# Final RMSNorm: two of nine row tiles scaled on GpSimd and ScalarE in place of VectorE

## The chip, the cores and the metric

One core of one Trainium2 chip. The metric is the device time of one execution in microseconds (us), the median of three runs. The whole program is one launch.

## The reference, cut to what matters

The program is one step of a decoder layer on 1024 prompt rows and 8 sample rows of width 1024: a mixer (pooling and retention), a mixture of 32 experts, and at the end the final norm of every row. All of it stays as it is; what the change touches is the last line:

```
x  = x + mixed @ w_out
x  = x + hier_moe(rmsnorm(x, g_ffn))
y  = rmsnorm(x, g_final)          # x * 1/sqrt(mean(x*x) + 1e-6) * g_final, per row
```

Each output row is the row times one number of its own (the inverse root of its mean square) times a vector of 1024 weights that is the same for all rows.

## The kernel before, in words

The 1032 rows are nine tiles: eight of 128 prompt rows and one of the 8 sample rows. `ORDER` (L576) takes the sample tile first, so that place n = 0 is the 8 rows and places 1 to 8 are prompt tiles 0 to 7. Up to the last stage the kernel is bound by TensorE's products in fp32 split in two parts. The experts' results are added row by row to `sum_d` in DRAM by indirect transfers that GpSimd (POOL) issues (L1415). When all of them have landed, POOL raises `parts_ready` (L1444), and the last stage begins:

- SyncE (SP) issues nine loads, `sum_d` to the tile of `x2` in SBUF, in the order n = 0 to 8 (L677 to L679), each with a semaphore of its own, `rows_in[n]`. Then SP issues the stores of the outputs in the order n = 0 to 8 (L680 to L684): before each it waits for `y_done`, which counts the scalings done. The last tile is stored in two halves of 512 columns. At the end SP waits for all stores (L685).
- ScalarE (ACT) squares each tile as it lands, with the row's sum of squares as a side result (L834, `Square`, output thrown away), and takes the square root of the means once for each group of tiles (L839, helper L354). The groups are `NORM_GROUPS` (L585): n = 0 to 2, 3 to 5, 6 and 7, and 8. `root3_done` counts the groups.
- VectorE (DVE) waits for a group's root, works out the inverse root in five short instructions on a few columns (`rsqrt_columns`, L163 to L167), and then scales the group's tiles in place: one `scalar_tensor_tensor` for each tile, (x times the row's number) times `gfin_b` (L1355, in `scale_rows`); the last tile takes two, by halves. `TAIL` (L586) is the list of these steps. `gfin_b`, the final weights on every partition, was loaded long before.
- POOL has nothing to do in this stage; TensorE neither.

Each engine executes its instructions in order; SP's queue also, so a store whose wait isn't met holds back all stores behind it.

Two places outside the last stage are needed to follow the prediction. In the mixer stage POOL multiplies 128x256 gates by 128x256 weights (L2182) and adds two 128x256 tiles (L2193), both `tensor_tensor` on fp32 in SBUF, while DVE forms the low parts of weights (L1915, `tensor_tensor` on two SBUF tiles of 128x512) or masks keys (L2136, L2138, the same operation on two SBUF tiles).

Of the kernel before, what the change touches and what calls it, by code (L numbers as in the profile page):

```python
# [25 lines left out]
F32 = mybir.dt.float32  # L26
# [4 lines left out]
ALU = mybir.AluOpType  # L31
ACT = mybir.ActivationFunctionType
AX = mybir.AxisListType.X

P = 128
D = 1024
KT = D // P
SEQ, NB, NTOK = 1024, 8, 1032
NT = 9
CH = SEQ // P  # L40
TC = NTOK // 3
H = 4
# [133 lines left out]
def step_kernel(nc, x_prompt, x_sample, state_pool, state_ret, g_mix, w_in, w_pool, pool_scale, ret_gn,  # L176
# [10 lines left out]
    with ExitStack() as ctx:  # L187
        def sem(name):
            return ctx.enter_context(nc.semaphore(name))
# [9 lines left out]
        small = whole.place("small", [P, 96], F32)  # L199
# [3 lines left out]
        at_W = whole.at  # L203
# [50 lines left out]
        x2 = rh.place("x2", [P, NT, D], F32)  # L254
# [82 lines left out]

        gfin_b = rc.place("gfin_b", [P, D], F32)
        junk_f = rc.place("junk_f", [P, D], F32)

        SS, MS, RS = 0, 9, 18
        HX, TX = 27, 36
# [9 lines left out]
        def root_of_means(act, a, b):  # L352

            return act.activation(small[:, MS + a:MS + b], small[:, SS + a:SS + b], ACT.Sqrt,  # L354
                                  bias=small[:, EPSC:EPSC + 1])
# [24 lines left out]
        rows_in = [sem(f"rows_in{t}") for t in range(NT)]  # L380
        raw_in = [sem(f"raw_in{i}") for i in range(3)]
        misc_in = sem("misc_in")
        gains_in = sem("gains_in")
# [14 lines left out]
        y_out = sem("y_out")  # L398
# [22 lines left out]
        S = {**by_pe, **by_act, **by_dve, **by_pool, **by_sp}  # L421
# [8 lines left out]
        def after(n):  # L430

            return max(n, 0) + 1 if isinstance(n, int) else n + 1

        def carried(eng, who):

            eng.sem_inc(carrier[who], 1)
# [28 lines left out]
        def is_first(t, n):  # L465
            return isinstance(t, int) and t < n
# [42 lines left out]
        def up_weights(sp, e, s):  # L509

            for j, w in enumerate((w1, w3)):
                sp.dma_start(w13[s][:, j, :, :].rearrange("p k f -> p (k f)"),
                             of_expert(w, e).rearrange("(p k) f -> p (k f)", p=P)).then_inc(w13_in[s], 16)

        def down_weights(sp, e, s):

            sp.dma_start(w2t[s][:, :, :].rearrange("p i n -> p (i n)"),
                         of_expert(w2, e).rearrange("(p i) n -> p (i n)", p=P)).then_inc(w2_in[s], 16)
# [4 lines left out]
        def blocks(eng, step):  # L523

            for s in range(ROUND):
                step(s, s, 0)
            with eng.Fori(1, ROUNDS) as g:
                for s in range(ROUND):
                    step(ROUND * g + s, s, g)
            for s in range(NE - ROUND * ROUNDS):  # L530
                step(ROUND * ROUNDS + s, s, ROUNDS)
# [5 lines left out]
        def expert_of(s, g):  # L537

            return 8 * (s % 4) + 2 * g + s // 4
# [36 lines left out]
        ORDER = [CH] + list(range(CH))  # L576

        def rows_of(n):
            return slice(0, NB if ORDER[n] == CH else P)

        def halves_of(n):

            return (slice(0, D),) if n < NT - 1 else (slice(0, 512), slice(512, D))

        NORM_GROUPS = ((0, 3), (3, 6), (6, 8), (8, 9))  # L585
        TAIL = [step for g, (a, b) in enumerate(NORM_GROUPS)  # L586
                for step in [("norm", g)] + [("scale", n) for n in range(a, b)]]

        def columns(t):

# [2 lines left out]
        def load_mixed(sp, t):  # L593
            s = t % 2
            if t >= 2:
                sp.wait_ge(S["ct_mm"], after(2 * (t - 1)))

            sp.wait_ge(mix_out[s], 16 * ((5 - s) * (H - 1) + 1) + 16 * (t // 2))
            if t == CH:
                sp.dma_start(mi[s][0:NB, :], mixed_d[SEQ:NTOK, :]).then_inc(mi_in[s], 16)  # L600
            else:
                sp.dma_start(mi[s][:, :], mixed_d[t * P:(t + 1) * P, :]).then_inc(mi_in[s], 16)

        def load_x(sp, t):
            s = t % 2
            if t >= 2:
                sp.wait_ge(S["x2_done"], after(2 * (t - 1)))
            if t == CH:
                sp.dma_start(xr[s][0:NB, :], x_s).then_inc(xr_in[s], 16)
            else:  # L610
                sp.dma_start(xr[s][:, :], x_p[t * P:(t + 1) * P, :]).then_inc(xr_in[s], 16)
# [14 lines left out]
        def stage_c_sp(sp):  # L626
            sp.wait_ge(S["sum_done"], after(9 * H))
            sp.dma_start(gffn_b[:, :], g_ffn[0:1, :].to_broadcast([P, D])).then_inc(route_in, 16)
            sp.dma_start(wr[:, :, 0:4], w_grp[0].rearrange("(k p) g -> p k g", p=P)).then_inc(route_in, 16)
            sp.dma_start(wr[:, :, 4:36], w_exp[0].rearrange("(k p) g e -> p k (g e)", p=P))\  # L630
                .then_inc(route_in, 16)
            sp.dma_start(gffn8[0:KT, :], g_ffn[0].rearrange("(k p) -> k p", p=P)).then_inc(route_in, 16)
            for t in range(2, CH + 1):
                if t < CH:
                    load_mixed(sp, t + 1)
                load_x(sp, t)

            def weights(b, s, g):

                if is_first(b, 2):  # L640
                    sp.wait_ge(S["wo_used"], after(b + 1))
                elif is_first(b, 3):
                    sp.wait_ge(S["w_mm"], after(NT))
                    sp.wait_ge(xg_in[0], 16)
                elif is_first(b, 4):
                    sp.wait_ge(S["h2_done"], after(NT))
                    sp.wait_ge(x2_out, 16 * NT)
                else:
                    sp.wait_ge(S["up_used"], after(KT * (b - SLOTS + 1)))
                    if not isinstance(b, int):  # L650
                        carried(sp, "sp")
                up_weights(sp, expert_of(s, g), s % SLOTS)
                if is_first(b, 1):
                    return
                if not is_first(b, SLOTS + 1):
                    sp.wait_ge(S["down_used"], after(4 * (b - SLOTS)))
                    if not isinstance(b, int):
                        carried(sp, "sp")
                down_weights(sp, expert_of((s - 1) % ROUND, g - (s == 0)), (s - 1) % SLOTS)

            sp.dma_start(gfin_b[:, :], g_final.unsqueeze(0).to_broadcast([P, D])).then_inc(gains_in, 16)
            blocks(sp, weights)
            sp.wait_ge(S["down_used"], after(4 * (NE - SLOTS)))
            down_weights(sp, expert_of((NE - 1) % ROUND, ROUNDS), (NE - 1) % SLOTS)

            def more(b, i):
                sp.wait_ge(S["down_used"], after(4 * b))
                carried(sp, "sp")
                e = sp.value_load(spill[0:1, bass.ds(i + SPILL, 1)], min_val=0, max_val=NE - 1)
                up_weights(sp, e, 0)  # L670
                down_weights(sp, e, 0)

            spilled(sp, more)


            sp.wait_ge(S["parts_ready"], after(1))
            for n, t in enumerate(ORDER):  # L677
                r = rows_of(n)
                sp.dma_start(x2[r, t, :], sum_d[t * P:t * P + r.stop, :]).then_inc(rows_in[n], 16)  # L679
            for n, t in enumerate(ORDER):  # L680
                dst = y_prompt[0, t * P:(t + 1) * P, :] if t < CH else y_sample.rearrange("b o d -> (b o) d")
                for half in halves_of(n):
                    sp.wait_ge(S["y_done"], after(n + 1 + half.start // 512))
                    sp.dma_start(dst[:, half], x2[rows_of(n), t, half]).then_inc(y_out, 16)  # L684
            sp.wait_ge(y_out, 16 * (NT + 1))  # L685


        def stage_c_act(act):
# [141 lines left out]
            for n in range(NT):  # L830
                r = rows_of(n)
                act.wait_ge(rows_in[n], 48 if n == CH else 32)
                act.wait_ge(S["sq3_done"], after(n))
                act.activation(junk_f[r, :], x2[r, ORDER[n], :], ACT.Square, scale=D ** -0.5,  # L834
                               accum_out=small[r, SS + n:SS + n + 1]).then_inc(S["sq3_done"], 1)
                for a, b in NORM_GROUPS:
                    if b == n + 1:
                        act.wait_ge(S["sq3_done"], after(b))
                        root_of_means(act, a, b).then_inc(S["root3_done"], 1)  # L839


        def three(pe, out, lhs, rhs, first, last):
# [525 lines left out]
        def stage_c_pool(pool):  # L1368
# [73 lines left out]
            for i in range(2):  # L1442
                pool.wait_ge(sum_out[i], 8 * NE)
            pool.sem_inc(S["parts_ready"], 1)  # L1444

        @block.sync
        def _(sp):
# [113 lines left out]
            tail(H - 1, lambda i: first_loads_c(sp, i))  # L1563
            sp.wait_ge(fixed_out, 16)
            stage_c_sp(sp)


# [15 lines left out]
        def _(act):  # L1583
# [125 lines left out]
            with act.Fori(1, H - 1) as h:  # L1709
                head(h, False, False)  # L1710
            head(H - 1, False, True)
            stage_c_act(act)


# [520 lines left out]
```

## Time and profile before

| | us |
|---|---|
| runs | 1058.55, 1060.94, 1061.08; median 1060.94 |
| profiled execution, its own time | 1059.97 |
| its span in the trace | 1058.2 |
| busy: TensorE, VectorE, ScalarE, GpSimd | 982.4, 739.5, 443.4, 217.7 |
| the last stage: first load issued, span's end | 1033.3, 1058.2 |

The profiled execution's own time is 1.8 us more than its span: what lies outside the first and last record. The last stage has no TensorE work, so the share of the whole says nothing of it; it is read from its own stretch of the trace.

### The profile page before, as it was taken

The page shows a single profiled execution, that of the slowest core. Times are in us where ns is not written, and L with a number is a line of the kernel's source. Part 1 is how long each engine was busy: PE and PEld are TensorE (multiplying, and loading weights), DVE is VectorE, ACT ScalarE, POOL GpSimd, SP SyncE. Part 2 cuts the span into 40 slices and gives each one's busy share as a digit, 9 for nine tenths or more (in the row PEclk, how much of TensorE's full clock was granted, in tenths as well). Part 3 has the DMA queues.
Part 4 walks back from the last instruction along what each step waited for, and adds up shares of the span by engine and source line. Part 5 has one row for each costly group of instructions (what it writes and reads, how often), then busy time and mean ns, then how long its engine had stood idle before and what let it go on. Part 6 is the DMA issues. An engine that isn't in the chain of part 4 may idle for free.

```text
span 1058.2 us, 16461 instructions
## 1 busy us (share of the span) xinstructions
PE 982.4 (93%) x5342; PEld 845.9 (80%) x5343; DVE 739.5 (70%) x1616; ACT 443.4 (42%) x738; POOL 217.7 (21%) x223
## 2 busy tenths in 40 slices
PE   5799999999989999999997999978999999999970
PEld 4798888988879888898875888857888888888850
DVE  5584457855568555684556555669999999999955
ACT  6422113011130111301112221136899888898854
POOL 0001221012200122011220000012444443454310
PEclk9899999999999999999998999989999999999995
DMA  7610205111051110501016443269999999999828
GB/s 251 227 30 26 65 21 168 41 39 52 26 162 41 34 57 26 172 31 60 11 64 220 165 160 119 103 242 386 388 391 401 393 393 390 393 395 388 299 35 324
DMA packets 74727, 190.24 MB, mean 180 GB/s; under 512 B 12503, under 2 KB 47555, under 8 KB 62227
## 3 DMA queue, kind: packets, MB, share of 16 engines
q1 hardware_dynamic: 61403, 159.66, 39.9%
q0 software_dynamic: 13248, 29.62, 9.6%
q8 instruction: 41, 0.67, 0.3%
q14 instruction: 35, 0.29, 0.1%
HBM read 167.43 MB, written 38.68 MB: 195 GB/s over the span
## 4 chain that ended last, share of the span: by engine, by line
PE 83%; DVE 8%; DMA 4%; issue 2%; ACT 1%; SPq 1%; DVEq 0%; POOLq 0%; ACTq 0%
PE bank L1866 17%; PE bank L844 11%; PE bank L846 11%; PE bank L845 11%; PE bank L871 10%; PE bank L1867 9%; PE bank L982 3%; PE bank L901 1%; PE bank L1749 1%; PE bank L1889 1%; DMA raw<-in_w_in_dram 1%; PE bank L1881 1%; PE bank L1877 1%; DMA hc<-const_head_tables_dram 1%; DVE x L1355 1%
## 5 line engine op out<-in xcount | busy, mean ns | idle before, releaser
L1233 DVE TENSOR_TENSOR w_lo<-w,w_hi 128x1024 fp32r<-128x1024 f32 x128 | 150.3, 1215 | 0.2 <-DVE vec L1195 0.2
L733 ACT ACTIVATE w_hi<-w 128x1024 fp32r<-128x1024 f32 x128 | 129.7, 1068 | 2.9 <-PE bank L846 2.9
L1866 PE MATMUL bank<-wvg_hi,hT_hi 128*128 128x512 f32 x256 | 104.3, 407 | 0.0
L844 PE MATMUL bank<-w_hi,xT_hi 128*128 128x512 f32 x256 | 102.9, 402 | 1.3 <-issue 1.3
L1866 PE MATMUL bank<-wvg_lo,hT_hi 128*128 128x512 f32 x256 | 101.0, 395 | 0.0
L1866 PE MATMUL bank<-wvg_hi,hT_lo 128*128 128x512 f32 x256 | 100.7, 393 | 0.0
L846 PE MATMUL bank<-w_hi,xT_lo 128*128 128x512 f32 x256 | 100.3, 392 | 0.0
L845 PE MATMUL bank<-w_lo,xT_hi 128*128 128x512 f32 x256 | 99.7, 390 | 0.0
L844 PE MATMUL bank<-hT_hi,wuqk_hi 128*128 128x344 f32 x288 | 95.4, 331 | 4.4 <-ACT line L1656 4.1
L1697 ACT ACTIVATE v<-bank 128x256 f32<-128x256 f32 x32 | 12.3, 383 | 201.2 <-PE bank L1867 201.2
L2193 POOL TENSOR_TENSOR mixed<-onorm,pgate 128x256 f32<-128x256 f32 x36 | 37.8, 1050 | 278.6 <-DVE onorm L2018 278.6
L845 PE MATMUL bank<-hT_lo,wuqk_hi 128*128 128x344 f32 x288 | 92.9, 323 | 0.0
L846 PE MATMUL bank<-hT_hi,wuqk_lo 128*128 128x344 f32 x288 | 92.7, 322 | 0.0
L2114 DVE SCALAR_TENSOR_TENSOR state<-state,small,bank 128x256 f32<-128x256 f32 x28 | 13.5, 480 | 109.2 <-PE bank L1889 109.0
L1238 DVE TENSOR_TENSOR w_lo<-w,w_hi 128x1024 fp32r<-128x1024 f32 x64 | 75.6, 1222 | 20.0 <-ACT w_hi L740 20.0
L1415 POOL DMA_INDIRECT sum_d<-y,icol x28 | 45.5, 1624 | 138.1 <-ACT y L770 125.3
L1867 PE MATMUL bank<-wvg_hi,hT_hi 128*128 128x256 f32 x256 | 71.8, 281 | 0.0
L1867 PE MATMUL bank<-wvg_hi,hT_lo 128*128 128x256 f32 x256 | 71.8, 280 | 0.0
L1867 PE MATMUL bank<-wvg_lo,hT_hi 128*128 128x256 f32 x256 | 71.8, 280 | 0.0
L2182 POOL TENSOR_TENSOR sg<-sg,gn_b 128x256 f32<-128x256 f32 x36 | 26.7, 741 | 191.5 <-ACT sg L1699 184.7
L740 ACT ACTIVATE w_hi<-w 128x1024 fp32r<-128x1024 f32 x64 | 64.6, 1066 | 0.0
L844 PEld LDWEIGHTS bank<-hT_hi,wuqk_hi 128*128 128x128 f32 x288 | 55.0, 191 | 8.0 <-ACT line L1656 4.7
(256 smaller groups left out, 2397.6 us busy)
## 6 DMA issues: line engine op xcount, KB each, us to landing
w<-in_w_dram SPq DMA_DIRECT2D x96, 1024.0 KB
raw<-in_w_in_dram SPq DMA_DIRECT2D x60, 256.0 KB, 3.2
xall<-in_x_prompt_dram SPq DMA_DIRECT2D x8, 512.0 KB, 7.0
mixed_d<-mixed POOLq DMA_DIRECT2D x32, 128.0 KB, 3.2
sample_state<-in_state_ret_dram SPq DMA_DIRECT2D x16, 256.0 KB, 3.6
out_dram<-sample_state SPq DMA_DIRECT2D x16, 256.0 KB, 4.4
mixed_in<-mixed_d SPq DMA_DIRECT2D x8, 512.0 KB, 4.3
x_again<-in_x_prompt_dram SPq DMA_DIRECT2D x8, 512.0 KB, 3.5
```

What stands on the lines that cost most here:

```text
L733: act.activation(hi, whole_w, ACT.Copy).then_inc(S["up_hi"], 1)
L740: act.activation(hi, whole_w, ACT.Copy).then_inc(S["down_hi"], 1)
L844: pe.matmul(out, lhs[0], rhs[0], start=first, stop=False)
L845: pe.matmul(out, lhs[0], rhs[1], start=False, stop=False)
L846: return pe.matmul(out, lhs[1], rhs[0], start=False, stop=last)
L871: mm = pe.matmul(banks[4 - 2 * s + n][:, :], mT[s][xi][:, k, :], wo[k][wi][:, n * 512:(n + 1) * 512], start=(k == 0 and xi + wi == 0), sto ...
L1233: dve.tensor_tensor(lo, whole_w, hi, ALU.subtract).then_inc(S["up_lo"], 1)
L1238: dve.tensor_tensor(lo, whole_w, hi, ALU.subtract).then_inc(S["down_lo"], 1)
L1415: pool.indirect_dma_start(out=sum_d, out_offset=bass.IndirectOffsetOnAxis(ap=index, axis=0), in_=yb[s2][:, :], in_offset=None, bounds_chec ...
L1866: g = pe.matmul(gates, x[xi], wvg[wi][:, 1:3, k, :], start=first, stop=last)
L1867: m = pe.matmul(v[:, 0:DV], x[xi], wvg[wi][:, 0, k, :], start=first, stop=last)
L2193: pool.tensor_tensor(mixed[s][:, :], onorm[:, :], pgate[:, :], ALU.add).then_inc(S["sum_done"], 1)
```

## The change

Tiles n = 3 and n = 4 (prompt tiles 2 and 3) leave DVE. POOL multiplies each, once its load has landed, by the final weights into a new buffer `by_g`, which lies where expert weights lay before; ACT multiplies it there by the row's inverse root, which DVE still works out with its group. ACT does so after its squares of all nine tiles, and waits until DVE has scaled four tiles (0, 1, 2 and 5), by which time the roots of the second group are there. DVE scales the other seven. The stores go in a new order: n = 0, 1, 2, 5, 6, 7, then 3 and 4 from `by_g`, then 8 in two halves. The loads keep their order.

```diff
+        by_g = nc.alloc_sbuf_tensor_at("x_by_gain", [P, 2, D], F32, offset=at_W)
+        BY_POOL = (3, 4)
+        STORED = [n for n in range(NT - 1) if n not in BY_POOL] + list(BY_POOL) + [NT - 1]
...
-                for step in [("norm", g)] + [("scale", n) for n in range(a, b)]]
+                for step in [("norm", g)] + [("scale", n) for n in range(a, b) if n not in BY_POOL]]
...
-            for n, t in enumerate(ORDER):
+            scaled = 0
+            for n in STORED:
+                t = ORDER[n]
                 dst = y_prompt[0, t * P:(t + 1) * P, :] if t < CH else y_sample.rearrange("b o d -> (b o) d")
+                if n in BY_POOL:
+                    i = BY_POOL.index(n)
+                    sp.wait_ge(S["sig_done"], after(9 * H + i + 1))
+                    sp.dma_start(dst, by_g[:, i, :]).then_inc(y_out, 16)
+                    continue
                 for half in halves_of(n):
-                    sp.wait_ge(S["y_done"], after(n + 1 + half.start // 512))
+                    scaled += 1
+                    sp.wait_ge(S["y_done"], after(scaled))
                     sp.dma_start(dst[:, half], x2[rows_of(n), t, half]).then_inc(y_out, 16)
...
+            for i, n in enumerate(BY_POOL):
+                act.wait_ge(S["y_done"], after(4))
+                act.wait_ge(S["sum_done"], after(9 * H + i + 1))
+                act.activation(by_g[:, i, :], by_g[:, i, :], ACT.Identity, scale=small[:, RS + n:RS + n + 1])\
+                    .then_inc(S["sig_done"], 1)
...
+            pool.wait_ge(gains_in, 32)
+            for i, n in enumerate(BY_POOL):
+                pool.wait_ge(rows_in[n], 32)
+                pool.tensor_tensor(by_g[:, i, :], x2[:, ORDER[n], :], gfin_b[:, :], ALU.mult).then_inc(S["sum_done"], 1)
```

## Rows read from the trace of the kernel before

**Rows 1.** The chain that ended last, its last pieces: start us, us, what

```profile
1034.12 4.37 DMA x<-sum_d
1038.51 1.16 ACT junk_f L834 x2
...
1040.97 3.66 DVE x L1355 x3
...
1045.42 3.68 DVE x L1355 x3
...
1049.86 2.48 DVE x L1355 x2
...
1053.10 0.75 DVE x L1355
1053.85 0.66 DVEq L187
```

**Rows 2.** Busy time by stretch of the last stage; last columns granted clock, DMA share, GB/s

```profile
1035.00:1041.00 6.00, 0.00 (x0) 0.00 (x0) 0.76 (x6) 4.55 (x8) 0.00 (x0) 0.50 0.99 384
1041.00:1046.00 5.00, 0.00 (x0) 0.00 (x0) 4.86 (x9) 4.61 (x10) 0.00 (x0) 0.50 1.03 415
1046.00:1051.00 5.00, 0.00 (x0) 0.00 (x0) 4.86 (x9) 2.26 (x6) 0.00 (x0) 0.50 1.02 415
1051.00:1052.00 1.00, 0.00 (x0) 0.00 (x0) 1.00 (x2) 0.00 (x0) 0.00 (x0) 0.50 0.76 307
...
1054.50:1055.00 0.50, 0.00 (x0) 0.00 (x0) 0.01 (x1) 0.00 (x0) 0.00 (x0) 0.50 0.74 279
...
1056.00:1056.50 0.50, 0.00 (x0) 0.00 (x0) 0.00 (x0) 0.00 (x0) 0.00 (x0) 0.50 0.29 111
```

**Rows 3.** The waits of SP's queue in the last 30 us: total, times, longest

```profile
SPq L684 <- DVE x L1355: 13.8, 10, 4.6
```

**Rows 4.** Timeline of the last stage: start us, us, engine, line, what

```profile
1028.96 1.55 POOL L1415 DMA_INDIRECT sum_d<-y,icol  x1 [7.84 <-ACT y L770]
...
1040.19 1.06 ACT L834 ACTIVATE junk_f<-x 128x1024 f32<-128x1024 f32 x1 [0.21 <-DMA x<-sum_d]
1040.38 0.16 DVE L165 TENSOR_TENSOR small<-small 128x3 f32<-128x3 f32 x1
...
1046.99 1.06 ACT L834 ACTIVATE junk_f<-x 128x1024 f32<-128x1024 f32 x1
```

**Rows 5.** Groups of the last stage by shape: busy us, mean ns, idle before

```profile
L1355 DVE SCALAR_TENSOR_TENSOR x<-x,small,gfin_b 128x1024 f32<-128x1024 f32 x7 | 8.6, 1277 | 0.1
L834 ACT ACTIVATE junk_f<-x 128x1024 f32<-128x1024 f32 x8 | 8.4, 1054 | 1.7 <-DMA x<-sum_d 1.2
```

**Rows 6.** Timelines of GpSimd and of VectorE in the mixer stage

```profile
80.92 0.72 POOL L2182 TENSOR_TENSOR sg<-sg,gn_b 128x256 f32<-128x256 f32 x1 [80.32 <-ACT sg L1699]
...
93.20 0.81 POOL L2193 TENSOR_TENSOR mixed<-onorm,pgate 128x256 f32<-128x256 f32 x1 [4.45 <-DVE onorm L2018]
93.33 1.23 DVE L1915 TENSOR_TENSOR wuqk_lo<-raw,wuqk_hi 128x512 fp32r<-128x512 f32 x1
...
244.47 0.68 DVE L1915 TENSOR_TENSOR wuqk_lo<-raw,wuqk_hi 128x512 fp32r<-128x512 f32 x1
244.51 1.23 POOL L2193 TENSOR_TENSOR mixed<-onorm,pgate 128x256 f32<-128x256 f32 x1 [5.14 <-DVE onorm L2018]
...
156.27 1.81 POOL L2193 TENSOR_TENSOR mixed<-onorm,pgate 128x256 f32<-128x256 f32 x1 [5.13 <-DVE onorm L2018]
156.28 1.23 DVE L2136 TENSOR_TENSOR kblk<-ks,misc 128x1024 fp32r<-128x1024 f32 x1
157.42 0.95 DVE L2138 TENSOR_TENSOR qm<-qT,misc 128x256 f32<-128x256 f32 x1
...
472.27 1.42 DVE L2102 SCALAR_TENSOR_TENSOR line<-line,small,line 128x1152 f32<-128x1152 f32 x1
472.80 1.48 POOL L2182 TENSOR_TENSOR sg<-sg,gn_b 128x256 f32<-128x256 f32 x1 [6.58 <-ACT sg L1699]
```

## The prediction

> **What bounds the kernel now.** I read the chain of waits first, for what the end hangs on, then the busy time by stretch for what else is full there, then the timeline. The last 25 us have no TensorE work. The chain runs through a load of rows until 1038.5, ACT's squares, and then DVE without a break: nine scalings in groups of three, three, two and the last halves, until 1054.51 [rows 1]. So DVE looks like the bound, and SP's stores wait for it, 13.8 us over ten waits [rows 3]. But the second view says that the transfers are nearly as full: DMA share 0.99 to 1.03 from 1035 to 1051, at 384 to 415 GB/s. Only two stretches show holes, 1051 to 1052 with a share of 0.76 and 1054.5 to 1055 with 0.74; most of the traffic is over by 1056.5 [rows 2]. Measured against the full share of 1.02, the holes are 0.26 and 0.14 us. One tile is 524,288 bytes, which at 415 GB/s is 1.26 us. DVE needs 1.28 us for a tile [rows 5]. Two resources are thus level here, and a lighter DVE can win no more than the holes.
>
> **What leaves DVE.** Two scalings of 128x1024. The second group of three took 3.68 us in a row [rows 1]; two thirds are 2.45 us. With nothing else in the way, the scaling of tile 6, the first of the third group, would end 2.45 us earlier than its 1049.86 + 1.24 = 1051.10. The short inverse-root instructions stay. The root of the third group would by then have to come from ACT, a little late; that is small and only counts where DVE gains time.
>
> **What POOL adds, and what it does to DVE.** POOL's two products of 128x1024 start when loads 3 and 4 have landed. ACT began the square of tile 3 at 1040.19, so load 3 is there at about 1040.1, just before DVE's first short instruction with two inputs in SBUF, L165 at 1040.38 [rows 4]. The trace has no POOL product of this size, but it has smaller ones beside DVE, and they don't run side by side. At 93.20 POOL's addition starts just before DVE's L1915, which then takes 1.23 us. At 244.47 the same L1915 comes first and takes 0.68, and now POOL's addition takes 1.23. At 156.27 POOL waits behind the whole 1.23 us of L2136 and takes 1.81, although DVE had its next instruction L2138 ready; that one is the late one. L2102, the operation of the final scaling with both tiles in SBUF, does it to POOL too: 1.48 us for a product that alone takes 0.72 [rows 6]. I read this as an exclusive turn: a POOL instruction and a DVE instruction that each read two SBUF tiles exclude each other for their length, and they alternate. DVE's scaling reads `x2` and `gfin_b`, both in SBUF.
>
> The Trainium skill, SBUF — State Buffer, section Who interferes with whom, says the same: a VectorE instruction with two SBUF inputs contends with a GpSimd instruction that reads SBUF, and the loser blocks fully. By that, the trace agrees (0.68 against 1.23 us for L1915).
>
> **How long one product holds DVE.** A 128x256 operation held L1915 up by 1.23 - 0.68 = 0.55 us [rows 6]. For 1024 columns in a row I take four times that, 2.2 us. Upper end: four times the whole 0.72 us that L2182 takes alone, 2.9 us. Lower end: POOL isn't faster than DVE with the same shape, 1.28 us [rows 5]. The value taken is nearest to a measured blocking and scales only its blocking part. The Trainium skill, GPSIMD Engine Reference, section 3.1 (Elementwise — side-by-side cycle accounting), gives 4497 ns for such an operation of 2048 columns; half is an estimate of 2.25 us, by which the sum below would be 0.1 us more; no run so far shows it.
>
> Both products fall into DVE's busy time: the first from 1040.2, the second right behind it, as load 4 lands some 1.3 us after load 3. Between them DVE gets a turn with one instruction. Whether that is L165 or the first scaling changes only the order. DVE loses 2 x 2.2 = 4.4 us and saves 2.45. The scaling of tile 6 ends at 1051.10 - 2.45 + 4.4 = 1053.05, that of tile 7 at about 1054.3, the last half at about 1056.5.
>
> **What ACT adds.** Two `Identity` of 128x1024 at the 1.05 us of a square [rows 5]. ACT's squares end at about 1048.2 [rows 4]. Its wait for four scalings ends with tile 5's: in the sum above some 2.0 us ahead of tile 6's end, at 1051.1. So the two tiles are ready at about 1052.3 and 1053.4. That is before SP gets to them, behind store 7 at 1054.3, so they cost nothing. If that cover were gone, the price would be at most the two, 2.1 us. Nothing else stands behind ACT's wait. `Identity` may need a table of functions; I count nothing, and it would lie before 1051.
>
> **The transfers.** The bytes stay; what changes is when each store may go. Stores 1, 2 and 5 are released late, and transfers run dry once the loads are over. When tile 6 is released at 1053.05, five tiles are still to be written: 6, 7, 3, 4 and 8. Tiles 3 and 4 were ready or nearly, but stand behind 6 and 7 in SP's queue. Five tiles at 1.26 us are 6.3 us, more than DVE and SP need to release them (8's second half is ready at 1056.5), so from 6 on the transfers are the bound. Of before: the last half was ready at 1054.51, the span ended at 1058.2, 3.69 us later, of which its own 0.63 are transfer; 3.06 us are start and completion. So the end is 1053.05 + 6.3 + 3.06 = 1062.4, and **the difference to the span of 1058.2 is +4.2 us**. The three new waits of SP and the new order cost nothing beyond that.
>
> The sum stands against the profiled execution of 1059.97: 1064.2. The median of the runs is 0.97 above that execution; between the two bases I take half, 1064.6. About 0.3% (3.2 us) is what a measurement of this kernel can tell from no change.
>
> **The rivals.**
> A, **the hold is short** (1.3 to 1.7 us per product): tile 6 would end at 1051.2 to 1052.0, the end at 1060.6 to 1061.4, +2.4 to +3.2 us, time 1062.4 to 1063.2 from the profiled execution. For it: POOL's 0.55 may hold a fixed part. Chance 0.20.
> B, **no exclusion in this stage**, the rival on the other side: POOL's products lie beside DVE's scalings at no cost, DVE ends early, and the transfers set the end. Then only the holes are won, 0.26 + 0.14, -0.4 us, 1059.6; even were transfers free, DVE's 2.45 us would be all, under 0.3%. It decides where DVE's scaling near 1041 stays at 1.28. Against it: all of [rows 6], L2102 above all. The Trainium skill has a rule for this side too: Advanced Engine Details and Errata, section VectorE Performance Modes, names only GpSimd and the 2p instructions of VectorE as blocking each other; a plain fp32 operation with two tiles would go free. The measured 1.23 speaks against it. Chance 0.12.
> C, **the hold is long** (2.9 us): tile 6 ends at 1054.4, the end is 1063.8, +5.6 us, 1065.6. Chance 0.08.
> That the change wouldn't do what it says has no good case: POOL has nothing after 1028.96 + 1.55 [rows 4], and the loads are the same.
>
> **How the numbers follow.** The forecast has 0.60. Slower by over 0.3%: nearly all of the forecast (0.56), C (0.08) and a little of A (0.02), 0.66. Faster by over 0.3%: only by chance of the runs, 0.03. The rest, 0.31, is within. The range takes in A's and C's bounds and the unrest of the runs (1058.55 to 1061.08): 1061.0 to 1067.5; B lies outside.
>
> **What would show it.** In the trace after: two POOL `tensor_tensor` of 128x1024 near 1040.2 and 1042.6, 2.2 to 2.5 us each where they don't wait; DVE instructions beside them, a short one or a scaling, drawn out by as much; DVE's last scaling ends near 1056.5 and not 1052; transfers with holes between 1045 and 1053 and full after; end near 1062.4. I am wrong if scalings beside POOL keep 1.28 us, if the transfers stay full throughout, or if the last store is not bound by those in front.

## The result, and the profile after

The changed kernel takes 1064.01 us in the median against 1060.94 before, 11 runs each: 3.07 us more; over all the runs the ratio is 1.0035 with a 95% interval of 1.0022 to 1.0048, slower. The forecast was 1064.6. The profiled execution took 1062.98 us with a span of 1061.3, against 1059.97 and 1058.2. All ratios here and below leave out one execution, of the variant with PSUM and the new place of stores 3 and 4, that took 1435.43 us at a granted clock of 0.65.

Spans hide one thing. The stages ahead of the last one, which no edit here touches, scatter: the first load of the last stage was issued anywhere from 1032.2 to 1036.2 us in the fourteen profiles of this study. So the last stage is also measured by itself, from the first load's issue to the span's end: 1058.2 - 1033.34 = 24.9 us before, 1061.3 - 1032.40 = 28.9 us after, +4.0 us; the forecast said +4.2. That the whole grew by only 3.1 is an earlier start of the stage in this execution, by 0.94 us.

The timeline of VectorE, GpSimd, ScalarE and SP in the last stage of the changed kernel (start us, us, engine, line; L1371 is the scaling that was L1355, L1464 GpSimd's product, L854 ScalarE's multiplication, L690 and L695 the stores):

```profile
1032.40 5.44 SPq L682 DMA_DIRECT2D x<-sum_d  x9
...
1040.16 3.66 DVE L1371 SCALAR_TENSOR_TENSOR x<-x,small,gfin_b 8x1024 f32<-8x1024 f32 x3
...
1040.52 7.82 POOL L1464 TENSOR_TENSOR x_by_gain<-x,gfin_b 128x1024 f32<-128x1024 f32 x2 [10.82 <-DMA x<-sum_d]
...
1044.46 1.60 DVE L163 TENSOR_SCALAR small<-small 128x3 f32<-128x3 f32 x1 [0.64 <-ACT small L357]
...
1046.17 2.19 DVE L165 TENSOR_TENSOR small<-small 128x3 f32<-128x3 f32 x1
...
1048.79 1.28 DVE L1371 SCALAR_TENSOR_TENSOR x<-x,small,gfin_b 128x1024 f32<-128x1024 f32 x1
...
1050.11 2.19 ACT L854 ACTIVATE x_by_gain<-x_by_gain,small 128x1024 f32<-128x1024 f32 x2 [1.69 <-DVE x L1371]
...
1050.84 2.48 DVE L1371 SCALAR_TENSOR_TENSOR x<-x,small,gfin_b 128x1024 f32<-128x1024 f32 x2
...
1053.72 1.35 SPq L690 DMA_DIRECT2D out_dram<-x_by_gain  x2
...
1054.07 1.42 DVE L1371 SCALAR_TENSOR_TENSOR x<-x,small,gfin_b 128x512 f32<-128x512 f32 x2
```

Two short instructions on three columns, 0.15 and 0.16 us before, now take 1.60 and 2.19. They are where VectorE stands while GpSimd reads SBUF. The scalings keep their 1.28 us in this execution: GpSimd's first product, asked for at 1040.52, waited until the three scalings were over at 1043.82. The two products in one group (min/median/max ns) agree with that:

```profile
L1464 POOL TENSOR_TENSOR x_by_gain<-x,gfin_b x2: 2346/3929/5512, 1040.5 to 1046.0; 128x1024 f32<-128x1024 f32 x2
```

One product takes 2.35 us; the other took 5.51, of which 3.3 are its wait behind the scalings, so that 2.2 are left for its work. The two together end at 1040.52 + 7.82 = 1048.34, and L165, the last instruction held, ends at 1048.36.

Where the time went is seen on the transfers (busy time by stretch, last columns granted clock, DMA share, GB/s), against [rows 2]:

```profile
1035.00:1041.00 6.00, 0.00 (x0) 0.00 (x0) 1.58 (x6) 3.60 (x8) 0.48 (x1) 0.50 0.92 350
1041.00:1046.00 5.00, 0.00 (x0) 0.00 (x0) 4.36 (x5) 4.61 (x10) 5.00 (x2) 0.50 1.03 416
1046.00:1051.00 5.00, 0.00 (x0) 0.00 (x0) 4.72 (x12) 3.25 (x7) 2.34 (x2) 0.50 0.37 152
1051.00:1052.00 1.00, 0.00 (x0) 0.00 (x0) 1.00 (x1) 1.00 (x2) 0.00 (x0) 0.50 0.98 410
1052.00:1054.00 2.00, 0.00 (x0) 0.00 (x0) 1.90 (x7) 0.29 (x1) 0.00 (x0) 0.50 0.61 250
1054.00:1056.00 2.00, 0.00 (x0) 0.00 (x0) 1.45 (x3) 0.00 (x0) 0.00 (x0) 0.50 1.01 406
```

Before, the share stood at 1.02 to 1.03 from 1041 to 1051. Now 5 us have 0.37 and 2 us have 0.61: against 1.02 that is 3.25 + 0.82 us of lost transfer time. The first stretch loses another 0.4 (0.92 for 0.99 over 6 us), and the 0.4 us of holes of before are gone. Together some 4.1 us, close to the stage's growth. The stretches are not quite the same part of the stage, as it began 0.94 us earlier here. The whole stage as one stretch, before and after, is free of that:

```profile
1033.34:1058.20 24.86, 0.00 (x0) 0.00 (x0) 13.85 (x30) 11.42 (x22) 0.00 (x0) 0.50 0.86 340
1032.40:1061.30 28.90, 0.00 (x0) 0.00 (x0) 15.01 (x28) 13.49 (x24) 7.82 (x2) 0.50 0.75 293
```

The full transfer time is 21.4 us in one and 21.7 in the other; the rest, time in which the transfers stand, grew by 3.7 us. The loss of the first stretch lies ahead of both products, and the second look at the changed kernel hasn't got it (from 2 to 8 us behind the first load's issue its share is 0.99, here 0.92), with a stage as long; it belongs to that execution and not to the change. SP's queue names who it waited for:

```profile
SPq L695 <- DVE x L1371: 14.2, 7, 5.9
```

Its longest wait, 5.9 us, is for tile 5, the one after tile 2. The stores of tiles 1 and 2 and of the next tile, after and then before:

```profile
1042.65 1.53 SPq L695 DMA_DIRECT2D out_dram<-x  x2
1050.10 0.33 SPq L695 DMA_DIRECT2D out_dram<-x  x1
...
1043.47 1.53 SPq L684 DMA_DIRECT2D out_dram<-x  x2
1046.73 0.33 SPq L684 DMA_DIRECT2D out_dram<-x  x1
```

Between these stores SP stood for 5.9 us, where it had been 1.7. The 4.6 us of before [rows 3] are another wait, the one for the first store (1042.27 - 1037.62, the end of the loads' issue at 1033.34 + 4.28).

### The profile page after: what moved, and what is told of

Read it like the earlier page. It is cut to its first block, busy times and chain, and to the rows that moved or that the text cites. A ratio compares the mean times of both kernels' runs of the same rounds, so it can differ in the third digit from the quotient of the medians.

```text
span 1061.3 us, 16466 instructions
## 1 busy us (share of the span) xinstructions
PE 979.9 (92%) x5342; PEld 843.9 (80%) x5343; DVE 740.1 (70%) x1614; ACT 445.9 (42%) x740; POOL 225.6 (21%) x225
## 4 chain that ended last, share of the span: by engine, by line
PE 80%; DVE 8%; DMA 5%; issue 3%; SPq 1%; ACT 1%; DVEq 0%; POOL 0%; POOLq 0%; ACTq 0%
PE bank L1886 17%; PE bank L860 11%; PE bank L862 11%; PE bank L861 11%; PE bank L887 9%; PE bank L1887 9%; PE bank L998 3%; PE bank L917 1%; DMA raw<-in_w_in_dram 1%; PE bank L1909 1%; PE bank L1901 1%; PE bank L1897 1%; DMA hc<-const_head_tables_dram 1%; PE bank L1769 1%; PE bank L1905 1%
## 5 line engine op out<-in xcount | busy, mean ns | idle before, releaser
L2213 POOL TENSOR_TENSOR mixed<-onorm,pgate 128x256 f32<-128x256 f32 x36 | 37.8, 1050 | 279.3 <-DVE onorm L2038 279.3
L1254 DVE TENSOR_TENSOR w_lo<-w,w_hi 128x1024 fp32r<-128x1024 f32 x64 | 75.6, 1221 | 20.0 <-ACT w_hi L751 19.5
```

Source lines behind the costliest of these rows:

```text
L1254: dve.tensor_tensor(lo, whole_w, hi, ALU.subtract).then_inc(S["down_lo"], 1)
L2213: pool.tensor_tensor(mixed[s][:, :], onorm[:, :], pgate[:, :], ALU.add).then_inc(S["sum_done"], 1)
```

## The experiments

The ratio is that of a kernel's time to the time of the one before on the same chip, 11 or 12 runs against 23 to 35 (11 against 11 for the changed kernel), with a 95% interval. Two executions of before, and one with nearly the same times on VectorE (products early), have stages of 24.9, 25.0 and 24.1 us, so a difference of under 1 us in that column can't be told from none. "Stage" is the last stage of the profiled execution. Tile 6 is the end of its scaling after the first load's issue, as the prediction's sum has it.

| kernel | ratio | interval | tile 6, us | stage, us |
|---|---|---|---|---|
| before | 1 | | 17.8 | 24.9 |
| before, once more | | one run | 18.1 | 25.0 |
| changed | 1.0035 | 1.0022 to 1.0048 | 19.7 | 28.9 |
| changed, once more | | one run | 19.7 | 28.9 |
| changed, stores 3 and 4 behind 5 | 1.0024 | 1.0010 to 1.0039 | 19.5 | 28.0 |
| before + products late | 1.0012 | 0.9997 to 1.0027 | 21.2 | 27.1 |
| before + products early | 0.9998 | 0.9984 to 1.0012 | 18.0 | 24.1 |
| changed, no products | 0.9993 | 0.9978 to 1.0009 | 16.2 | 25.4 |
| changed, weights in PSUM | 1.0021 | 1.0005 to 1.0036 | 18.2 | 26.6 |
| changed, one tile | 1.0006 | 0.9993 to 1.0020 | 18.7 | 25.9 |
| PSUM and stores 3, 4 behind 5 | 1.0015 | 1.0002 to 1.0028 | 16.7 | 25.2 |
| before, new order of stores | 1.0018 | 1.0006 to 1.0029 | 18.4 | 26.8 |
| tiles 1 and 2 | 1.0027 | 1.0015 to 1.0040 | 18.7 | 27.4 |
| tiles 1 and 2, stored early | 1.0005 | 0.9992 to 1.0019 | 18.7 | 26.0 |

### Is it GpSimd's products? Added alone, late and early

```diff
+        by_g = nc.alloc_sbuf_tensor_at("x_by_gain", [P, 2, D], F32, offset=at_W)
...
 pool.sem_inc(S["parts_ready"], 1)
+pool.wait_ge(gains_in, 32)
+for i in range(2):
+    pool.wait_ge(rows_in[3 + i], 32)
+    pool.tensor_tensor(by_g[:, i, :], gfin_b[:, :], gfin_b[:, :], ALU.mult).then_inc(S["sum_done"], 1)
```

The early ones leave out the wait for `rows_in`.

> The kernel before, with two GpSimd products of 128x1024 added (gfin_b times gfin_b, result unused) that start when loads 3 and 4 have landed; VectorE scales all nine tiles as before, the stores are as before. Theory of the hold: VectorE ends 3.5 to 4.4 us later, and the time is +3.5 to +4.4 us. Rival of the order of stores, or of ScalarE's part: 0.

> The same two added products, without the wait for the loads: they run in the 7 us in which VectorE still waits for the first root. Theory of the hold: no VectorE instruction is drawn out, time 0 (within 0.5 us) against before. If instead GpSimd's traffic as such (against the loads, for instance) costs time, +1 us or more.

The late ones, in the timeline:

```profile
1040.10 3.74 POOL L1449 TENSOR_TENSOR x_by_gain<-gfin_b 128x1024 f32<-128x1024 f32 x2 [10.01 <-DMA x<-sum_d]
1040.17 1.84 DVE L166 TENSOR_TENSOR small<-small 128x3 f32<-128x3 f32 x1
1042.04 1.82 DVE L167 SCALAR_TENSOR_TENSOR small<-small 128x3 f32<-128x3 f32 x1
1043.89 3.66 DVE L1356 SCALAR_TENSOR_TENSOR x<-x,small,gfin_b 8x1024 f32<-8x1024 f32 x3
```

The early ones:

```profile
1033.27 3.74 POOL L1448 TENSOR_TENSOR x_by_gain<-gfin_b 128x1024 f32<-128x1024 f32 x2 [2.79 <-DMA sum_d<-y,icol]
...
1040.58 0.16 DVE L166 TENSOR_TENSOR small<-small 128x3 f32<-128x3 f32 x1
1040.78 0.16 DVE L167 SCALAR_TENSOR_TENSOR small<-small 128x3 f32<-128x3 f32 x1
```

The same two instructions of GpSimd cost VectorE 2 x 1.67 us where they meet its work and nothing where it waits anyway. That pair shows the hold as the products' effect, and that the early ones, which run beside the loads, cost nothing that can be measured (ratio 0.9998). Two parts of the expectation missed. A product that reads one tile twice takes 1.87 us and not 2.35 (3.74 for both), so the hold is shorter; VectorE ended 3.4 us later. And the end moved by only 2.3 us of stage and 1.3 us of time, with an interval that takes in no change. The end came 2.6 us behind the last scaling and not 3.7 as before. A smaller backlog of transfers in front of the last half would do that; it is the likely reason, and no run tests it by itself.

### The change without the products

```diff
-            for i, n in enumerate(BY_POOL):
-                pool.wait_ge(rows_in[n], 32)
-                pool.tensor_tensor(by_g[:, i, :], x2[:, ORDER[n], :], gfin_b[:, :], ALU.mult).then_inc(S["sum_done"], 1)
...
-                act.wait_ge(S["sum_done"], after(9 * H + i + 1))
-                act.activation(by_g[:, i, :], by_g[:, i, :], ACT.Identity, scale=small[:, RS + n:RS + n + 1])\
+                act.activation(by_g[:, i, :], x2[:, ORDER[n], :], ACT.Identity, scale=small[:, RS + n:RS + n + 1])\
```

This kernel leaves the final weights out for tiles 3 and 4.

> The changed kernel without GpSimd's two products: ScalarE multiplies tiles 3 and 4 by the row's number straight from x2, and the final weights are left out for these two tiles. Order of stores, ScalarE's waits and work stay. Theory of the hold: VectorE's instructions are no longer drawn out, tile 6 is scaled at 15.6 us after the first load, the transfers are the bound and the time is that of before within 0.5 us. Rival of the order or of ScalarE: +3 us stays.

```profile
1043.67 0.17 DVE L163 TENSOR_SCALAR small<-small 128x3 f32<-128x3 f32 x1
1043.75 0.17 DVE L164 RECIPROCAL small<-small 128x3 f32<-128x3 f32 x1
1043.95 0.16 DVE L165 TENSOR_TENSOR small<-small 128x3 f32<-128x3 f32 x1
```

The short instructions are short again, and with them the loss is gone: ratio 0.9993, stage 25.4. ScalarE's wait for four scalings, its two multiplications and the new order of the stores, are all still in it. VectorE's last scaling ends 1051.78 - 1032.18 = 19.6 us after the first load, against 1054.51 - 1033.34 = 21.2 before, and the interval around the time still takes in none. So 1.6 us off VectorE's end gained nothing here. But this run also has the new order of the stores, and a hole of its own:

```profile
1048.00:1050.00 2.00, 0.00 (x0) 0.00 (x0) 1.93 (x6) 1.69 (x2) 0.00 (x0) 0.50 0.60 246
```

Against 1.02 that is 0.8 us. The share is 1.01 and 1.03 from 1050 to 1054, so what ends the stage is transfers. What the two tiles would be worth without such a hole, no run shows; from the rows of before it is at most the holes there, 0.4 us. Taking this run's 0.8 us off its stage of 25.4 gives 24.6, within the scatter of before. Either is too little to measure in the time.

### One product in place of two

```diff
-BY_POOL = (3, 4)
+BY_POOL = (4,)
```

> The changed kernel with one tile (n = 4) on GpSimd and ScalarE in place of two. Theory: one hold of 2.2 us in place of two; tile 6 is scaled at 18.0 us after the first load, and four tiles of 1.26 us stand to be written: +1.3 us against before. Rival (a cost that doesn't go with the number of products, such as a wait or the first use of an instruction): +3 us stays, or nearly.

```profile
1042.62 5.23 POOL L1464 TENSOR_TENSOR x_by_gain<-x,gfin_b 128x1024 f32<-128x1024 f32 x1 [11.10 <-DMA x<-sum_d]
...
1045.57 2.30 DVE L163 TENSOR_SCALAR small<-small 128x3 f32<-128x3 f32 x1
```

One hold of 2.1 us in place of two, stage 25.9, +1.0 us for +1.3 expected; the ratio of 1.0006 can't be told from none. The cost goes with the number of products. That one costs less than half of two (+1.0 against +4.0 us) fits the fewer stores that wait behind, but no run shows this by itself.

### The order of the stores, with and without the products

```diff
-STORED = [n for n in range(NT - 1) if n not in BY_POOL] + list(BY_POOL) + [NT - 1]
+STORED = [0, 1, 2, 5, 3, 4, 6, 7, 8]
```

> The changed kernel with stores 3 and 4 right behind store 5, before 6 and 7. Theory (GpSimd's two products hold VectorE up by 2.2 us each, and late stores end in a full queue of transfers): VectorE's times stay as in the changed kernel; only the hole in the transfers between the stores 5 and 6 is filled; from store 5's release at 17.7 us after the first load, six tiles of 1.26 us and 3.06 us of start and completion give 28.3 us of stage where the changed kernel has 28.9: some 0.6 us less than the changed kernel, still +3 us against before. Rival (the new order of the stores alone is the cause, since tiles 3 and 4 stand behind 6 and 7): the 3 us come back, 0 against before.

In this execution load 3 was there by the first of VectorE's short instructions, L163, which began with the product at 1039.31:

```profile
1039.31 4.68 POOL L1464 TENSOR_TENSOR x_by_gain<-x,gfin_b 128x1024 f32<-128x1024 f32 x2 [9.48 <-DMA x<-sum_d]
...
1039.59 2.11 DVE L165 TENSOR_TENSOR small<-small 128x3 f32<-128x3 f32 x1
1041.74 2.27 DVE L166 TENSOR_TENSOR small<-small 128x3 f32<-128x3 f32 x1
```

This is the course that the prediction had drawn: products at once, L165 and L166 held. VectorE was just as late in the end (tile 6 at 19.5), and the new place of stores 3 and 4 gave 0.9 us of stage back, for 0.6 expected. In the time the two can't be told apart (1.0010 to 1.0039 against 1.0022 to 1.0048), but most of the cost is still there, so the order isn't the whole cause. The second run puts the new order into the kernel before, where VectorE scales everything:

```diff
-for n, t in enumerate(ORDER):
+for n in (0, 1, 2, 5, 6, 7, 3, 4, 8):
+    t = ORDER[n]
```

> The kernel before, VectorE scaling all nine tiles in its order, with only the stores in the order of the changed kernel: 0, 1, 2, 5, 6, 7, 3, 4, 8. Tests the sum of the queue by itself: transfers run dry while stores 3 and 4 stand behind, tile 6 is released at 17.8 us after the first load, five tiles of 1.26 us and 3.06 us follow: +2.2 us against before. If the queue of stores doesn't matter, 0.

```profile
1048.00:1051.00 3.00, 0.00 (x0) 0.00 (x0) 2.86 (x7) 2.88 (x6) 0.00 (x0) 0.50 1.01 414
1051.00:1054.00 3.00, 0.00 (x0) 0.00 (x0) 2.86 (x8) 0.85 (x3) 0.00 (x0) 0.50 0.33 134
```

Ratio 1.0018, stage 26.8 (+1.9 us for +2.2): with VectorE's work untouched (tile 6 at 18.4, 0.6 later than before, 0.41 of it a wait for a root), stores 3 and 4 standing behind 5, 6 and 7 dry the transfers out (share 0.33). So the order has a price of its own, of the same kind as late scalings. It is not to be added to the hold's: without the products the same order cost nothing that the time shows; tile 6 was then early (16.2). Both work through one thing, when the next store in SP's queue may go.

### Which input excludes

```diff
+            dve.wait_ge(S["parts_ready"], after(1))
+            for i in range(2):
+                dve.tensor_copy(banks[2 + i][:, :], gfin_b[:, 512 * i:512 * i + 512]).then_inc(S["gain_ready"], 1)
+            dve.wait_ge(S["gain_ready"], after(2))
...
-                for half in halves_of(n):
+                for i in range(2):
+                    half = slice(512 * i, 512 * i + 512)
...
-                                             in1=gfin_b[r, half], op0=ALU.mult, op1=ALU.mult)\
+                                             in1=banks[2 + i][r, :], op0=ALU.mult, op1=ALU.mult)\
```

The counts that SP and ScalarE wait for are doubled to match, as each tile now takes two scalings. The second run also has the stores in the order 0, 1, 2, 5, 3, 4, 6, 7, 8.

> The changed kernel with VectorE's copy of the final weights in PSUM (two banks, copied while VectorE waits), so that each scaling reads one tile from SBUF and one from PSUM; each tile takes two scalings of 512 columns. Theory (the exclusion is by the second SBUF input): GpSimd's first product runs beside scalings 1 and 2 without drawing them out, and only the short instructions on the small columns still wait, about 1 us in all; scalings take about 0.75 us for 512 columns, so the end is +1.7 us against before, 2.3 us less than the changed kernel's stage. Rival (any VectorE instruction excludes GpSimd): both products still hold VectorE by 2.2 us each or wait for it, and with the halves' own cost of 1.5 us it is +4 us or more.

> Both mendings: VectorE's weights in PSUM and stores 3 and 4 behind store 5. Theory: with tile 5 released at about 14.9 us after the first load, the transfers are full from there on, +0.7 us against before, not faster than before. If VectorE were what bounds the kernel before, the two tiles taken from it would show as a gain of 1 to 2 us.

The timeline of the second of these:

```profile
1041.58 4.67 POOL L1469 TENSOR_TENSOR x_by_gain<-x,gfin_b 128x1024 f32<-128x1024 f32 x2 [10.55 <-DMA x<-sum_d]
1041.59 4.03 DVE L1372 SCALAR_TENSOR_TENSOR x<-x,small,bank 8x512 f32<-8x512 f32 x6
...
1045.55 0.72 DVE L163 TENSOR_SCALAR small<-small 128x3 f32<-128x3 f32 x1
```

Six half scalings in 4.03 us, 0.67 each, run through while GpSimd makes both products in 4.67, twice its undisturbed 2.35. Neither waits for the other. With weights in SBUF the same two engines took turns. So for the scalings it is the second SBUF input that excludes. It isn't the only thing that does: L163 was still drawn out, to 0.72, and it has a single SBUF input. It ends with the products (1045.55 + 0.72 = 1046.27 against 1041.58 + 4.67 = 1046.25). In the first of the two runs GpSimd came a little earlier and L167, with two inputs, took 2.23 us; the six half scalings behind it took 4.03 us beside GpSimd there too:

```profile
1040.21 4.66 POOL L1469 TENSOR_TENSOR x_by_gain<-x,gfin_b 128x1024 f32<-128x1024 f32 x2 [10.50 <-DMA x<-sum_d]
1040.35 2.23 DVE L167 SCALAR_TENSOR_TENSOR small<-small 128x3 f32<-128x3 f32 x1
```

The stages took 26.6 and 25.2 us, where 26.6 and 25.6 were expected (+1.7 and +0.7 against 24.9); the ratios, 1.0021 and 1.0015, are no gain in either. With two tiles less on VectorE and hardly any hold, the kernel isn't faster than before. The expectation had the transfers full from tile 5 on; they weren't, as the stores of tiles 3 and 4 went only at 1050.8, behind ScalarE's multiplications:

```profile
1050.00:1052.00 2.00, 0.00 (x0) 0.00 (x0) 2.00 (x6) 1.83 (x2) 0.00 (x0) 0.50 0.52 213
```

That is 1.0 us of transfer time. A version without this hole wasn't run.

### Other tiles

Tiles 1 and 2, whose loads come first:

```diff
-BY_POOL = (3, 4)
+BY_POOL = (1, 2)
```

with stores 0, 3, 4, 5, 1, 2, 6, 7, 8 and ScalarE's wait for one scaling.

> The changed kernel with tiles 1 and 2 on GpSimd and ScalarE in place of 3 and 4, so that GpSimd's products run mostly before VectorE starts; stores in the order 0, 3, 4, 5, 1, 2, 6, 7, 8. Theory: the second product holds VectorE's first short instructions up by about 1.6 us, no scaling is held; but no store but the small one may go before tile 3 is scaled at 13.4 us after the first load, and the transfers run dry at 12; eight tiles from 13.4 with 3.06 us of start and completion end at 26.5 us of stage, +1.7 us against before. Rival (the hold is all there is): with only 1.6 us held and 2.5 us saved, a gain of up to 0.9 us.

> As the one before, but ScalarE multiplies tiles 1 and 2 right after the second group's root, between its squares, and the stores go in the order 0 to 8. Theory: the transfers stay full from 12 us on, VectorE is no longer late, and the stage takes some 25.2 us: 0 to +0.5 us against before, no gain although VectorE has two tiles less, since the transfers are the bound. If VectorE were the bound before, -1 to -2 us.

In the second one ScalarE multiplies both tiles behind the second group's root, and the stores go in the order 0 to 8.

The timeline of the second one:

```profile
1037.94 4.64 POOL L1465 TENSOR_TENSOR x_by_gain<-x,gfin_b 128x1024 f32<-128x1024 f32 x2 [7.02 <-DMA x<-sum_d]
...
1040.70 1.91 DVE L163 TENSOR_SCALAR small<-small 128x3 f32<-128x3 f32 x1 [16.32 <-ACT small L357]
...
1045.67 2.17 ACT L855 ACTIVATE x_by_gain<-x_by_gain,small 128x1024 f32<-128x1024 f32 x2
1045.79 0.17 DVE L163 TENSOR_SCALAR small<-small 128x3 f32<-128x3 f32 x1 [1.21 <-ACT small L357]
```

L163 ends at 1042.61, the products at 1042.58. Only 1.75 us of hold are left here. The first still cost 1.0027 (stage +2.5 for +1.7: VectorE also waited 1.38 us for the second root). The second is level with before (1.0005), stage 26.0 for 25.2 expected; the transfers, expected full, have a hole where store 1 waited for ScalarE:

```profile
1046.00:1047.00 1.00, 0.00 (x0) 0.00 (x0) 0.86 (x5) 1.00 (x2) 0.00 (x0) 0.50 0.45 172
1047.00:1048.00 1.00, 0.00 (x0) 0.00 (x0) 1.00 (x2) 1.00 (x2) 0.00 (x0) 0.50 0.41 168
```

No version that was run beats the kernel before.

### Once more

> The changed kernel once more, for one more look at which instruction of VectorE waits for GpSimd's products. Theory: if load 3 lands before VectorE's short instructions with two inputs, these are held as in the run with the new store order; if it lands behind them, GpSimd waits for the three scalings and the next group's short instructions are held. Either way the stage takes 28 to 29 us.

> The kernel before once more, for the scatter of the last stage by itself: 24.0 to 25.0 us from the first load's issue to the span's end.

```profile
1042.95 8.03 POOL L1464 TENSOR_TENSOR x_by_gain<-x,gfin_b 128x1024 f32<-128x1024 f32 x2 [10.52 <-DMA x<-sum_d]
1042.96 5.80 DVE L1371 SCALAR_TENSOR_TENSOR x<-x,small,gfin_b 8x1024 f32<-8x1024 f32 x3
...
1048.70 2.30 DVE L163 TENSOR_SCALAR small<-small 128x3 f32<-128x3 f32 x1
```

And from the groups by shape:

```profile
L1371 DVE SCALAR_TENSOR_TENSOR x<-x,small,gfin_b 8x1024 f32<-8x1024 f32 x1 | 3.4, 3411 | 0.0
```

A third course: GpSimd came 0.01 us ahead of the first scaling, which was held (3.41 us for 1.27), and the second product then waited until all three were over. The stage is 28.9 us, as in the first execution; before's second look has 25.0. With the run that has stores 3 and 4 behind 5, these are three courses of the two engines, and tile 6 is as late in each.

## Why the prediction was right

**The bound of before.** Right as far as the runs go: the transfers were full, and less work on VectorE gained nothing that can be measured. The run without products has the whole relief and none of the hold, and it came out at 0.9993, with an interval from 0.9978 to 1.0009. It also has the new order and 0.8 us of hole, so the bound itself rests on the rows of before, and this run agrees with it.

**The hold.** The exclusive turn was right, and so was its size: 2.2 us for 1024 columns, as four times the 0.55 of 256 columns [rows 6]; measured were 2.03 us on L165, 2.35 for the product's own record, 2.1 on L163 with one tile. Rival A (1.3 to 1.7 us) would hold only for a product that reads one tile twice, rival C (2.9 us) nowhere. Rival B fell with the drawn-out L163 and L165, though not by the sign that the prediction gave for it. That sign, a scaling near 1041 that keeps its 1.28 us, did come in the profiled execution: there GpSimd was the one that waited. Read by the letter it would have spoken for B; the length of GpSimd's own record, 5.51 us for 2.35, is what decides. In the second look the scaling was the one held, 3.41 us. The rule of the Trainium skill, SBUF — State Buffer, section Who interferes with whom, that a VectorE instruction with two SBUF inputs contends with GpSimd's reads, is borne out by the pair of SBUF and PSUM weights. That of Advanced Engine Details and Errata, section VectorE Performance Modes, which names only the 2p instructions, would have let L165 go: 2.19 us against 0.16 speak against it.

**A step that was wrong.** "They alternate", and that between the products VectorE gets one instruction and GpSimd the next. Between scalings that follow each other without a gap GpSimd got no turn: it waited through all three of the first group in the changed kernel, with one tile on GpSimd (5.23 us for 2.35), and, with its second product, in the second look. It came on at the short instructions behind. The prediction's start at 1040.2 was off too: in the profiled execution load 3 landed 1.3 us later after the first load's issue than assumed. Neither changed the end, as the prediction said of the order: in the three courses seen, tile 6 came at 19.5, 19.7 and 19.7 us.

**The sum for VectorE.** It said 4.4 us lost, 2.45 saved, tile 6 later by 1.95. Measured: 1.44 + 2.03 = 3.5 us of hold, 0.64 of wait for a root, and tile 6 at 19.68 against 17.76 after the first load, +1.92. Of what is left, 1.92 + 2.45 - 3.5 - 0.64 = 0.2 us, 0.12 is the first root, which came at 6.88 for 6.76 us. So that the sum met 1.92 with 1.95 is luck in part, by two terms that cancel: the hold cost 0.9 us less, because VectorE was waiting for ScalarE when the first product held it, and that wait was not in the sum.

**The queue.** Tile 6 at 19.68 + 6.3 for five tiles + 3.06 gives 29.0; measured 28.9. With five tiles at other times it gives 25.6 without the products (25.4 measured), but 27.5 with weights in PSUM (26.6) and 27.7 in before's new order (26.8); with one tile on GpSimd, four tiles at 18.7, it gives 26.8 (25.9). The 3.06 us, read from one execution, was up to 1 us too much: two executions with the same times on VectorE, before and with early products, ended 24.9 and 24.1 us after their first load was issued. That the sum met the stage to 0.1 us is luck within that; that it met the size isn't. The mechanism, stores released late and then five tiles in a full queue, is what the stretches show: 0.37 and 0.61, then 1.01.

**ScalarE's part.** Right: `Identity` took 1.13 to 1.15 us, for 1.05 assumed, and no table was loaded for it. Both tiles were ready at 1052.3 and SP came to them at 1053.7. The wait for tile 5 was the later of ScalarE's two.

Over all the runs the change cost 0.35%, which is 3.7 us (3.07 between the medians), a little under the 4.2 of the sum.

## What to carry to other kernels

Before work is moved off the engine that ends a stage, look whether something else is as full: here the transfers were, at a share of 1.02, and two tiles less on VectorE gained nothing that could be measured. GpSimd is no free engine beside VectorE where both read two tiles from SBUF; here products in VectorE's idle time cost nothing, and products in its busy time held one of its instructions each for about 2 us, even one on three columns. And in a queue that is served in order, a store that waits sets the time of all behind it: put it where it will be ready.

## What the runs showed of the hardware

- The exclusion reaches a `tensor_scalar` on a 128x3 tile with one SBUF input: L163 took 1.60, 2.30 and 0.72 us beside GpSimd's products, 0.15 to 0.17 without, and each time ended within 0.1 us of the product. The prediction had counted only instructions with two inputs. The Trainium skill, SBUF — State Buffer, section Who interferes with whom, lists `tensor_scalar` among the operations that can take the pair of ports shared with GpSimd, and the trace agrees (1.60 us for 0.16).
- GpSimd's product of 128x1024 fp32 takes 2.35 us with two different tiles and 1.87 with the same tile twice.
- The exclusion of a scaling hangs on where its second input lies: 3.41 us for 1.27 beside GpSimd with both in SBUF, and 0.67 us for each half, not drawn out, with one in PSUM.
- A waiting GpSimd instruction got no turn between back-to-back scalings (two boundaries in each of three executions), though it did get one between two different instructions, L2136 and L2138 [rows 6]. What decides the turn is open; no run was made for it.
